# Three edits of the expert layer of an encoder block: gate stores in four pieces, 72 instead of 64 table tiles beside the gates, three token tiles held in PSUM in the values' stage

## The reference, cut to what matters

```python
q = (xt @ wq).reshape(T, 8, 2, 128)
s = einsum('thpe,hpke->thpk', q, keys)
sv, si = top_k(s, 16)                       # per head, per key half
cand = sv[:, :, 0, :, None] + sv[:, :, 1, None, :]
tv, ti = top_k(cand, 16)                    # 16 experts per head, 128 per token
g = softmax(tv)
a = einsum('cd,ced->ce', x, utab[eidx])     # x . u of each picked expert
out = einsum('ce,ced->cd', g * gelu(a), vtab[eidx])
x = layer_norm(alpha * x + (1 + g2) * out)
```

## Time and profile before

| | us |
|---|---|
| median of 3 runs | 4294.86 (4288.96 to 4295.96) |
| the profiled execution's own time | 4303.32 |
| its span | 4301.5 |
| TensorE busy in the span | 3764.7 (88%) |
| DVE busy | 2871.9 (67%) |
| ACT busy | 977.2 (23%) |
| POOL busy | 1302.5 (30%) |
| mean granted TensorE clock | 0.937 of full |

### The profile page before, as it was taken

How to read it: one execution, slowest core, us unless ns; L and a number is a source line. 1 busy time by engine, 2 the same in 40 slices (tenths; PEclk the granted TensorE clock), 3 DMA queues, 4 the chain that set the end, 5 groups by cost and what they waited for, 6 DMA issues and landing times. The chain is left out here.

```text
span 4301.5 us, 57936 instructions
## 1 busy us (share of the span) xinstructions
PE 3764.7 (88%) x19170; PEld 3289.1 (76%) x19170; DVE 2871.9 (67%) x6317; ACT 977.2 (23%) x1361; POOL 1302.5 (30%) x805
## 2 busy tenths in 40 slices
PE   6889899997879798999987776777758999999997
PEld 3579788886757688999986776776757888888885
DVE  5562133224544315788778897988859888888898
ACT  1111122221132211222322222222222222222221
POOL 1132112112312112332333232323215544454450
PEclk9789999998989899999998898988889999999998
DMA  4741212216542223333349989898998787888784
GB/s 183 282 138 41 84 60 80 75 62 223 195 173 96 83 83 102 122 131 119 129 152 259 241 268 236 271 240 258 244 249 319 288 296 287 286 292 300 276 308 153
DMA packets 501996, 826.29 MB, mean 192 GB/s; under 512 B 288455, under 2 KB 309191, under 8 KB 495720
## 3 DMA queue, kind: packets, MB, share of 16 engines
q1 hardware_dynamic: 111848, 370.03, 24.8%
q0 software_dynamic: 84096, 318.80, 20.8%
q10 hardware_dynamic: 305856, 135.28, 13.1%
HBM read 679.31 MB, written 144.70 MB: 192 GB/s over the span
## 5 line engine op out<-in xcount | busy, mean ns | idle before, releaser
L2049 POOL DMA_INDIRECT va_rows<-in_vtab,k_pick x256 | 500.5, 1955 | 531.6 <-DVE k_big L2176 436.5
L79 PE MATMUL va_fps<-va_vt_h,va_c_h 128*128 128x512 f32 x1536 | 601.2, 391 | 53.8 <-DVE va_vt_l L2152 51.4
L80 PE MATMUL va_fps<-va_vt_l,va_c_h 128*128 128x512 f32 x1536 | 600.1, 391 | 0.0
L81 PE MATMUL va_fps<-va_vt_h,va_c_l 128*128 128x512 f32 x1536 | 599.7, 390 | 0.0
L79 PE MATMUL ga_aps<-k_u_h,k_ut_h 128*128 128x384 f32 x1024 | 382.4, 373 | 116.2 <-DVE k_ut_l L1953 112.2
L1941 DVE TENSOR_SCALAR ga_first<-ga_iota,k_sel,ga_gs 128x128 f16<-128x128 f16 x1536 | 427.9, 353 | 33.0 <-issue 33.0
L79 PEld LDWEIGHTS va_fps<-va_vt_h,va_c_h 128*128 128x128 f32 x1536 | 289.9, 189 | 116.9 <-DVE va_vt_l L2152 52.5
L80 PE MATMUL ga_aps<-k_u_l,k_ut_h 128*128 128x384 f32 x1024 | 367.8, 359 | 0.0
L81 PE MATMUL ga_aps<-k_u_h,k_ut_l 128*128 128x384 f32 x1024 | 366.8, 358 | 0.0
L79 PE MATMUL se_aps<-k_u_h,k_ut_h 128*128 128x384 f32 x1024 | 343.8, 336 | 15.2 <-POOL k_ut_l L1619 15.2
L80 PE MATMUL se_aps<-k_u_l,k_ut_h 128*128 128x384 f32 x1024 | 343.2, 335 | 0.0
(11 more groups left out here) (293 smaller groups left out, 8173.6 us busy)
## 6 DMA issues: line engine op xcount, KB each, us to landing
k_ut<-in_utab SPq DMA_DIRECT2D x129, 512.0 KB, 3.3
va_vt<-in_vtab SPq DMA_DIRECT2D x128, 512.0 KB, 6.7
va_c<-scratch_ahead SPq DMA_DIRECT2D x128, 384.0 KB, 4.8
va_wt<-scratch_gates SPq DMA_DIRECT2D x128, 384.0 KB, 5.6
hy_tab<-in_tab POOLq DMA_DIRECT2D x64, 512.0 KB, 5.1
sp_wada<-in_w_ada SPq DMA_DIRECT2D x24, 1024.0 KB, 8.8
scratch_ahead<-se_gelu_a ACTq DMA_DIRECT2D x64, 384.0 KB, 2.4
scratch_ahead<-ga_gelu_a ACTq DMA_DIRECT2D x64, 384.0 KB, 4.6
```

The costliest lines, as they stand in the source:

```text
L79: nc.tensor.matmul(out, w[0], x[0], start=first, stop=False)
L80: nc.tensor.matmul(out, w[0], x[1], start=False, stop=False)
L81: return nc.tensor.matmul(out, w[1], x[0], start=False, stop=last)
L2049: nc.gpsimd.indirect_dma_start(got[:, q % SLOTS_G, :], None, vrows, picked(K, q)).then_inc(got_in[q % SLOTS_G], 16)
```

## The change

It edits three stages.

*Select and gates.* `AT` goes from 8 to 7, so that 56 table tiles are computed beside selection and 72 beside the gates; the Exp moves from table tile 6 of 8 to table tile 4 of 7 (counted from 0). In the gates' stage a turn is 18 table tiles, 48 groups and 64 gathered rows, and there are 4 turns; each table tile has 2 or 3 groups. The ACT program is written out without a loop. A full buffer of `wide` is stored in four pieces of 32 key rows (4096 descriptors, 768 KB each), one piece after the `ahead` store of each following table tile. The last block is stored in three pieces at the end, as before. The DVE program also makes the low part of table tile 72.

*Values.* Token tiles 0 to 2 (`STAY`) keep a pair of banks each and sum in PSUM over all 32 groups. Token tiles 3 to 5 pass through the fourth pair one after the other, and DVE adds them to SBUF as before. On TensorE passing and staying tiles alternate. `turn` has adds only for t = 0, 1, 2 and none at its end. The staying tiles' residual at the end is one instruction and not two.

```diff
-AT = 8
+AT = 7
...
-                        if j == AT - 2:
+                        if j == AT - 3:
                             act.wait_ge(e_in, n + 1)
...
-        TURNS = BESIDE // 4
-        SIDE = GATHERED * PICKS // BESIDE
+        TURNS = 4
+        TILES = BESIDE // TURNS
+        GROUPS = DENSE // G // TURNS
+        ROWS = GATHERED * PICKS // TURNS
+        BLOCK = TW // G
...
+            waiting = []
+            for n in range(BESIDE):
+                i, q, a = n // TILES, n % TILES, n % 2
+                split(1 - a, n + 1, n // 2)
+                act.wait_ge(act_stored[a], 16 * (n // 2 + 1))
+                todo = list(groups_of(q))
+                for h in range(2):
+                    gelu(a, n, h)
+                    for b in (todo[:-1], todo[-1:])[h]:
+                        m = GROUPS * i + b
+                        if m % BLOCK == 0 and m // BLOCK >= 2:
+                            hold(act, K, stored[m // BLOCK % 2], 16 * PIECES * (m // BLOCK // 2))
+                        scatter_out(m)
+                        if m % BLOCK == BLOCK - 1 and m // BLOCK < BLOCKS - 1:
+                            waiting += [(m // BLOCK, c, m) for c in range(PIECES)]
+                act.wait_ge(gelu_ok, 2 * n + 6)
+                act.dma_start(S["ahead"][n + FIRST], gelu_a[:, a, :]).then_inc(act_stored[a], 16)
+                if waiting:
+                    block, c, m = waiting.pop(0)
+                    act.wait_ge(act_out, m + 5)
+                    store(block, NK // PIECES * c, NK // PIECES * (c + 1), stored[block % 2])
...
+            with dve.Fori(0, TURNS) as i:
+                for q in range(TILES):
+                    for b in groups_of(q):
+                        one_hot(GROUPS * i + b, b % 4)
+                        for j in rows_after(b):
+                            dot(i, j)
+                    low(1 - q % 2, TILES * i + q + 1)
...
+        STAY = DT // 2
+        FINAL = [STAY, 0, STAY + 1, 1, STAY + 2, 2]
...
+        def banks(tt):
+            pair = tt if tt < STAY else STAY
+            return fps[:, 2 * pair:2 * pair + 2, :]
...
+            def passing(s, g, j):
+                pe.wait_ge(f_ok, STAY * g + j + 1)
+                for h in range(2):
+                    for t in range(GT):
+                        last = part(s, t, STAY + j, h, t == 0, t == GT - 1)
+                return last.then_inc(f_mm, 1)
...
+            def group(s, g):
+                ready(g)
+                for j in range(STAY):
+                    passing(s, g, j)
+                    last = staying(s, j, False)
+                last.then_inc(group_mm, 1)
...
+            def add_sums(g, j):
+                hold(dve, K, f_mm, STAY * g + j + 1)
+                row = sums[:, GATHERED + STAY + j, :]
+                v.tensor_tensor(row, row, wide_banks(STAY), ALU.add).then_inc(f_ok, 1)
...
                 for t in range(GT):
                     coefficients(g + 1, t)
-                    add(t)
+                    if t < STAY:
+                        add(t)
                     coef_low(1 - s, g + 1, t)
                     value_low(1 - s, g + 1, t)
                     for j in range(take * t, take * t + take):
                         take_row(start, j, isinstance(start, int) and start == 0 and j < GATHERED)
-                for tt in range(GT, DT):
-                    add(tt)
```

More of the change, by code:

```diff
@@ L1893, in gelu @@
                 nc.scalar.activation(gelu_a[:, a, h * DH:(h + 1) * DH], aps[:, 2 * a + h, 0:DH], ACT.Gelu).then_inc(gelu_ok, 1)
[L1895 to L1918, removed]
+            def store(block, lo, hi, done):
+                act.dma_start(S["gates"].rearrange("i j t -> j i t")[:, lo:hi, block * TW:(block + 1) * TW],
+                              wide[block % 2][:, lo:hi, :]).then_inc(done, 16)
+            waiting = []
[3 more added lines that the diff above has]
+                act.wait_ge(act_stored[a], 16 * (n // 2 + 1))
+                todo = list(groups_of(q))
+                for h in range(2):
+                    gelu(a, n, h)
+                    for b in (todo[:-1], todo[-1:])[h]:
+                        m = GROUPS * i + b
[10 more added lines that the diff above has]
+                    store(block, NK // PIECES * c, NK // PIECES * (c + 1), stored[block % 2])
@@ L1919, in _ @@
+            assert not waiting
+            act.wait_ge(act_out, BLOCKS * BLOCK + 4)
+            for c, (lo, hi) in enumerate(((0, 2), (2, 8), (8, NK))):
+                store(BLOCKS - 1, lo, hi, K["last_gates"][c])
+            act.wait_ge(stored[0], 16 * PIECES * (BLOCKS // 2))
+            act.wait_ge(stored[1], 16 * PIECES * (BLOCKS // 2 - 1))
             for s in range(2):
@@ L2052, in _, with part, staying @@
         def _(pe):
-            pe.sem_inc(f_mm, 2 * DT)
-            def part(s, t, tt, bank, h, first, last):
-                return product3(nc, fps[:, 2 * bank + h, :],
+            pe.sem_inc(group_mm, 2)
+            def part(s, t, tt, h, first, last, into=None):
+                return product3(nc, banks(tt if into is None else into)[:, h, :],
                                 (c_h[:, s, t, tt * P:(tt + 1) * P], c_l[:, s, t, tt * P:(tt + 1) * P]),
                                 (vt_h[:, s, t, half(h)], vt_l[:, s, t, half(h)]), first, last)
[L2060 to L2066, removed]
+            def passing(s, g, j):
[4 more added lines that the diff above has]
+                return last.then_inc(f_mm, 1)
+            def staying(s, tt, last_group):
+                for h in range(2):
+                    for t in range(GT):
+                        last = part(s, t, tt, h, False, last_group and t == GT - 1)
+                return last
             def ready(g):
@@ L2070, in ready @@
                 pe.wait_ge(c_lo, GT * g + GT + 2)
-            for some in (range(0, BP), range(BP, DT)):
-                for t in range(GT):
[L2074 to L2082, removed]
+            def group(s, g):
[4 more added lines that the diff above has]
+                last.then_inc(group_mm, 1)
+            pe.wait_ge(f_ok, 1)
+            for t in range(GT):
+                pe.wait_ge(vt_ok, t + 3)
+                pe.wait_ge(c_lo, t + 3)
+                for tt in [STAY] + list(range(STAY - 1)):
+                    for h in range(2):
+                        last = part(0, t, tt, h, t == 0, tt == STAY and t == GT - 1)
+                    if tt == STAY and t == GT - 1:
+                        last.then_inc(f_mm, 1)
+            for h in range(2):
+                passing(0, 0, h + 1)
+                for t in range(GT):
+                    last = part(0, t, STAY - 1, h, t == 0, False)
+            last.then_inc(group_mm, 1)
             group(1, 1)
@@ L2085, in _, with both @@
                 for s in range(2):
-                    ready(2 * i + s)
                     group(s, 2 * i + s)
             ready(BODY)
[L2089 to L2093, removed]
-            ready(BODY + 1)
[L2095 to L2101, removed]
+            pe.wait_ge(f_ok, STAY * BODY + 1)
+            for h in range(2):
+                for t in range(GT):
+                    part(0, t, STAY, h, t == 0, False)
+            for tt in range(STAY):
+                staying(0, tt, False)
+            ready(BODY + 1)
+            def both(tt, into):
                 for h in range(2):
@@ L2104, in _ @@
                         for t in range(GT):
-                            last = part(s, t, tt, tt % BP, h, s == 0 and t == 0, s == 1 and t == GT - 1)
-                last.then_inc(f_mm, 1)
+                            last = part(s, t, tt, h, s == 0 and t == 0, s == 1 and t == GT - 1, into)
+                return last
+            staying(1, STAY, True).then_inc(done_mm, 1)
+            staying(1, 0, True).then_inc(done_mm, 1)
+            pe.wait_ge(done_ok, 1)
+            both(STAY + 1, STAY).then_inc(done_mm, 1)
+            staying(1, 1, True).then_inc(done_mm, 1)
+            pe.wait_ge(done_ok, 2)
+            both(STAY + 2, 0).then_inc(done_mm, 1)
+            staying(1, 2, True).then_inc(done_mm, 1)
         @block.scalar
@@ L2206, in _ @@
             gate2 = K["ada_row"][:, 2:4, :].rearrange("p a b -> p (a b)")
             def residual(k):
[L2209 to L2214, removed]
@@ L2229, in _ @@
             hold(dve, K, row_used, GATHERED * PICKS + SLOTS_G)
-            for k in range(DT, KT):
+            for k in range(GT, KT):
                 residual(k)
```

85 lines of the change are left out of this document (45 added, 40 removed).

## The result

The changed kernel takes 4332.26 us (median of 4 runs, 4326.86 to 4335.32) against 4291.91 us of the kernel before in the same session: ratio 1.0091, 95% interval 1.0074 to 1.0108. It is slower, by 40 us or 0.9%; 4321 was forecast. Its profiled execution took 4335.32 us with a span of 4333.5, 32.0 above the span before.

A forecast was written before the change was run, and what follows sets the result against it. TensorE was taken to bound select and the values' stage, no engine the gates' stage, where a big store held ACT. -65 - 93 + 131 + 58 - 5 = +26 on the 4294.9 us median gave 4321 us, range 4265 to 4385.

The forecast's parts named there:

- Select: Select stage: one table tile less per token tile and DVE's wait for the Exp gone, -65 us.
- Gates: Gates' stage: stall behind the big store gone, nine low parts added, some time put back for DMA, -93 us.
- the 9 us put back for transfers: Gates' stage: 9 us of the gain given back because DMA was already busy 0.92 of the stage.
- The 22 us taken off DVE's waits for issue: Gates' stage: two thirds of DVE's 33.0 us of waits for issue, once per block, would go: -22 us.
- The pause: Values' stage: TensorE idles before groups 2 to 30 for low parts behind the last add, 4.4 or 5.6 us each, +131.
- The clock: Values' stage: TensorE runs at half clock after each of 29 pauses, losing 2.0 us each time, +58 us.
- The rival that had the clock stay up: Values' stage: pauses come but the clock stays up, 4263 us, faster than before; chance 0.12.
- The upper bound of 3.4 us per pause: Values' stage: most that the low clock could cost after each pause, 3.4 x 29 = 99 us.
- The tail: End of the values' stage: shorter TensorE pause before group 31, four more residual instructions on DVE, -5 us, between -10 and 0.
- transfers are not the bound of the gates' stage: Judges a rival: transfers bound the gates' stage, which then gives only -50, total 4364 us; chance 0.17.
- four pieces do free the queue: Judges a rival: in the gates' stage pieces still block the next `ahead` store's issue, 4381 us; chance 0.05.
- the cover does not hold: Judges a rival: in the values' stage DVE has step 3's low parts early, no pause comes, 4132 us; chance 0.04.

The follow-up runs named there:

- loads_first: Changed kernel, but at the end of the values' stage SP loads the last two value tiles before it waits for residuals: 4325.96 us, 1.0081 of the kernel before.
- rows_later: Changed kernel with only the two gathered rows of step 2 taken at the end of step 3, the add left in place: 4231.58 us, 0.9855 of the kernel before.
- old_values: Changed kernel's select and gates' stages with the values' stage of the kernel before: 4133.52 us, 0.9615 of the kernel before.

## Why the prediction was right

The mechanism of both halves was right: the store that held ACT's queue, and the add that stands ahead of the low parts. That the sum came so near is in part luck, for its misses have both signs: -3.9 in select, -4.8 in gates and +14.7 in the values' stage, +6.0 for the spans. The medians differ by 40.4 us, 8.4 more than the spans: the profiled execution of the kernel before is 11.4 us above its median, that of the changed kernel 3.1.

- *Select*, -65: measured -68.9, of which 2.3 us were there at its first gelu (1679.7 before, 1677.4 after). DVE's wait for the Exp is gone.
- *Gates*, -93: measured -97.8. No wait for the rounded tile is left, and DVE waits for no gathered row: of the 9 us put back for transfers about half was too much. The 22 us taken off DVE's waits for issue had the wrong cause. They were laid to the store because they came once per block, but in the kernel before a block is also one turn of DVE's loop. Now there are fifteen blocks stored in pieces and four turns, and the waits come at the start of the three later turns:

```profile
DVE ga_second L1956 <- issue: 10.5, 3, 3.7
DVE ga_first L1958 <- issue: 8.1, 3, 2.7
```

  The first pair is at 2364 us, the others some 217 us, one turn, behind each other. 18.6 of the 33.0 us are left, so 14 went where I took off 22. That fewer turns took them away fits this, but no run changed the turns alone.
- *The pause*, 26 x 4.4 + 3 x 5.6 = +131: in the trace 4.34 us idle (and some 0.16 by which the next matmul would have overlapped), 5.46 to 5.53 in the edge turns.
- *The clock*, 29 x 2.0 = +58: work at 0.50 for 5.3 and 3.1 us in turn, half of it lost, a mean of 2.1. The rival that had the clock stay up is out. From group 1 to group 30 the stage takes 191.7 us more than before; pauses and clock were forecast at 189. The upper bound of 3.4 us per pause came from a row read wrong: in the 6.80 us at 0.50 of the earlier trace rows TensorE worked only 4.20, so 2.1 us were lost there.
- *The tail*, -5: this term failed, and by its sign. TensorE began group 30 at 4231.1; from there it took 102.4 us to the end, 96.8 before: +5.6. The pause before group 31 did shrink, from 12.18 to 7.73 us, but the pause of 8.62 us for token tile 3's pair is new. The step I missed is SP's queue. I counted the residuals that moved on DVE and not that SP waits for them in program order, ahead of the last two value tiles' loads. In loads_first the tail takes 92.9 us, 3.9 less than before and near the forecast, although the second pause stays.
- The 14.7 us by which the values' stage was missed are the tail (10.6), the start (1.4) and the pauses (2.7).
- *Rivals*: transfers are not the bound of the gates' stage (share 1.01, DVE 97% busy); four pieces do free the queue, two would not have; the cover does not hold.
- Two small sums are off and move nothing: DVE's work per table tile is (838.7 + 10)/72 = 11.8 us and not 11.7, and a stage of 860 us would be 109 below 969 and not 107.

## What to carry to other kernels

An instruction that waits for the slow engine should stand behind everything that the slow engine's next step needs. Fewer instructions on an engine that is not the bound gained nothing here; the order they leave behind may lose a lot, and it costs twice when the clock falls with the pause. A long store of small descriptors held the engine that issued the next one on its queue: cut it until the trace shows that the next issue is no longer held, counting the pieces that queue up behind one another. When a step is moved, look at every queue that waits for it, SP's too. And when a wait comes once per something, ask what else comes as often.

## What the hardware showed unexpected

The clock fell at pauses of 1.95 us too, in 11 of 29 (rows_later), between which TensorE was busy without a gap; in the kernel before, the two pauses of 2.15 and 2.40 us at the stage's start had not done that, and in old_values the one of 2.40 us did. At 4.34 us it fell in all 26. So at about 2 us the pause's length alone does not settle it.

The stores of a block of gates (16384 descriptors of 192 bytes) took 22 to 27 us or 32 to 35 us in the kernel before, two of the one and two of the other in turn, by the times of their packets. It goes with the place in the row of 3072 bytes: block k begins at byte 192 k, and the seven of the fifteen blocks that took 22 to 27 us are those whose 192 bytes cross no multiple of 256. That is read off one kernel; another place was not tried.
